# Out-projection tiles grouped 1 0 4, 3 5 8, 2 6 7, and the first up step cut at column 256

## What is computed

```python
mix = concat([gmlp_out, attn])                     # (tokens, 1024)
mix = einsum('bte,ed->btd', mix, w_out)            # out-projection
x = layer_norm(DEEPNORM_ALPHA * x + mix, ln1_g, ln1_b)
up = einsum('btd,df->btf', x, w_up)                # 1024 -> 2 * 2816
hc = conv_b + sum(conv_w[i] * hp[:, i:i + T] for i in range(3))
g, u = hc[..., :D_FF], hc[..., D_FF:]
y = einsum('btf,fd->btd', gelu(g) * u, w_down)     # followed by a second layer_norm
```

## Time and profile before

| what | value |
|---|---|
| median of 3 runs | 2336.68 us (2334.15 to 2340.17) |
| the profiled execution | 2335.85 us, its span 2334.1 us |
| TensorE matmul busy in the span | 2217.3 us (95%) |
| VectorE, ScalarE, GpSimd busy | 1657.2 (71%), 981.3 (42%), 825.8 us (35%) |
| the chain that ended last, by engine | TensorE 73%, VectorE 15%, ScalarE 4% |

### The profile page before, as it was taken

How to read it: one execution, slowest core, us unless ns; L and a number is a source line. 1 busy time by engine, 2 the same in 40 slices (tenths; PEclk the granted TensorE clock), 3 DMA queues, 4 the chain that set the end, 5 groups by cost and what they waited for, 6 DMA issues and landing times.

```text
span 2334.1 us, 35859 instructions
## 1 busy us (share of the span) xinstructions
PE 2217.3 (95%) x14276; PEld 2012.1 (86%) x14276; DVE 1657.2 (71%) x2014; ACT 981.3 (42%) x1773; POOL 825.8 (35%) x444
## 2 busy tenths in 40 slices
PE   7999899799999999999999998988999999999996
PEld 7997677799999998888798976768999999987885
DVE  1568747788878786787636697477787777767676
ACT  3226735444344334344322376454334434443342
POOL 1115234544554450220311342354455455311311
PEclk9999989899999999999999999998999999999998
DMA  5312146122222225765552213541232222365762
GB/s 154 95 34 65 55 147 185 44 84 84 83 61 85 85 67 175 252 218 194 176 135 47 58 39 106 150 153 47 80 88 60 86 85 67 107 234 189 243 214 90
DMA packets 207974, 269.50 MB, mean 115 GB/s; under 512 B 31952, under 2 KB 166584, under 8 KB 207736
## 3 DMA queue, kind: packets, MB, share of 16 engines
q1 hardware_dynamic: 207808, 267.21, 37.3%
HBM read 217.39 MB, written 46.13 MB: 113 GB/s over the span
## 4 chain that ended last, share of the span: by engine, by line
PE 73%; DVE 15%; ACT 4%; DMA 3%; issue 2%; POOL 2%; SPq 1%; ACTq 0%; DVEq 0%; POOLq 0%
PE ps L2059 35%; PE ps L1773 14%; PE ps L1738 9%; PE ps L1998 6%; DVE rl L1423 2%; DMA wrow<-in_w_down 1%; DVE bnst L1252 1%; PE ps L1798 1%; PE ps L1877 1%; PE ps L1903 1%; DVE bt L1335 1%; PE ps L1892 1%; DVE cb L1496 1%; PE ps L1856 1%; DVE rzc L1238 1%
## 5 line engine op out<-in xcount | busy, mean ns | idle before, releaser
L2059 PE MATMUL ps<-bt,bh 128*128 128x272 f32 x3520 | 591.7, 290 | 19.7 <-issue 16.0
L2059 PEld LDWEIGHTS ps<-bt,bh 128*128 128x128 f32 x3520 | 501.8, 190 | 20.8 <-issue 20.8
L938 ACT ACTIVATE bh<-wblk 128x512 fp32r<-128x512 f32 x308 | 183.6, 624 | 511.4 <-POOL wblk L745 260.8
L2059 PE MATMUL ps<-bt,bl 128*128 128x272 f32 x1760 | 366.4, 290 | 0.0
L2059 PEld LDWEIGHTS ps<-bt,bl 128*128 128x128 f32 x1760 | 277.1, 190 | 0.0
L733 POOL TENSOR_TENSOR bl<-wblk,bh 128x512 fp32r<-128x512 f32 x98 | 164.1, 1677 | 302.4 <-ACT bh L938 302.4
L1773 PE MATMUL ps<-rh,ah 128*128 128x512 f32 x792 | 247.2, 393 | 9.5 <-DVE ah L1434 5.8
L1773 PE MATMUL ps<-rl,ah 128*128 128x512 f32 x792 | 245.2, 391 | 0.0
L2059 PE MATMUL ps<-ba,bh 128*128 128x272 f32 x1408 | 235.7, 290 | 4.7 <-DVE gu L1378 2.8
L1355 DVE TENSOR_TENSOR bl<-wblk,bh 128x512 fp32r<-128x512 f32 x210 | 171.8, 850 | 85.4 <-ACT bh L938 85.4
L1423 DVE TENSOR_TENSOR rl<-wrow,rh 128x1024 fp32r<-128x1024 f32 x132 | 191.5, 1452 | 50.8 <-ACT rh L994 50.3
(11 more groups left out here) (223 smaller groups left out, 4091.8 us busy)
## 6 DMA issues: line engine op xcount, KB each, us to landing
wrow<-in_w_down SPq DMA_DIRECT2D x132, 512.0 KB, 4.6
wblk<-in_w_up SPq DMA_DIRECT2D x88, 512.0 KB, 5.2
a_scr<-hg SPq DMA_DIRECT2D x44, 552.0 KB, 3.4
araw<-a_scr SPq DMA_DIRECT2D x88, 192.0 KB, 4.3
wrow<-in_w_out SPq DMA_DIRECT2D x48, 256.0 KB, 5.4
wrow<-in_w_out SPq DMA_DIRECT2D x24, 512.0 KB, 4.6
wraw<-in_w_in SPq DMA_DIRECT2D x10, 1024.0 KB, 5.9
z_scr<-rzc SPq DMA_DIRECT2D x16, 512.0 KB, 4.7
```

Source lines behind the costliest of these rows:

```text
L938: act.activation(bh[b][:], block_of(f, b), ACT.Copy).then_inc(S["u_hi"], 1)
L2059: e = nc.tensor.matmul(out[:, n, :], lhs, rhs[:, HW_ // 2 * n:HW_ // 2 * n + HW_ // 2], start=(k == 0 and m == 0), stop=(k == HK - 1 and m ...
```

## The change

The groups become (1, 0, 4), (3, 5, 8), (2, 6, 7), so the last group holds one tile that needs a single operand and two that need four subtractions. `M_OPS` and `M_AT` follow: the first two pieces of the input are three tiles' in four pieces instead of two, tiles 2 and 3 go in one piece. In the first up step the 544 columns are cut at 256 instead of 272: columns 0 to 255 of all operands come from tiles 0, 1, 4, 5 and the samples alone. The products' first parts (12 matmuls of 256 columns) are issued ahead of what the last three tiles are needed for, their second parts (12 of 288) behind it. The second tile of the last group is turned into banks 4 and 5. ScalarE brings the first tile back ahead of the root for the third; VectorE's subtractions and low parts of the last group are put in another order; c11 goes ahead of the last three low parts; the sum for block S4 goes behind the low part of block S2 on GpSimd; `B_11` of step 1 waits for c21 instead of c22, since the banks are other ones. Each layer does all of it once.

```diff
-C3 = [(0, 1, 2), (3, 4, 8), (5, 6, 7)]
+C3 = [(1, 0, 4), (3, 5, 8), (2, 6, 7)]
...
 def up_bank(f, product):
+    if f == 0 and product in (B_S3, B_22):
+        return 6 if product == B_S3 else 2
     return 2 * ((7 * f + product) % 3)
+def z_bank(t):
+    return 4 if t == C3[2][1] else 6
...
-M_OPS = [(4, 8, 0, 3), (0, 4, 0, 3), (0, 8, 3, 4), (0, 8, 4, 5), (0, 8, 5, 8), (0, 8, 8, 9)]
+M_OPS = [(4, 8, 0, 2), (4, 8, 4, 5), (0, 4, 0, 2), (0, 4, 4, 5), (0, 8, 2, 4), (0, 8, 5, 8), (0, 8, 8, 9)]
...
+        def up_half(f, product, n):
+            bank, cut = up_bank(f, product), up_cut(f)
+            if f == 0:
+                return ps[:, bank, 512 - cut:512] if n == 0 else ps[:, bank + 1, 0:HW_ - cut]
+            return ps[:, bank + n, 0:HW_ // 2]
```

In GpSimd's queue:

```diff
-                for b in (B_S1, B_S2, B_S4):
-                    sum_up(l, 0, b)
-                for b in (B_S2, B_S1, B_22):
-                    lo_up(l, 0, b)
+                sum_up(l, 0, B_S1)
+                sum_up(l, 0, B_S2)
+                lo_up(l, 0, B_S2)
+                sum_up(l, 0, B_S4)
+                lo_up(l, 0, B_S1)
+                lo_up(l, 0, B_22)
```

In ScalarE's queue, behind the last group:

```diff
                 deviation(l, 0, t1)
                 normal(l, t1)
+                turned(l, t0)
                 deviation(l, 0, t2)
                 normal(l, t2)
-                turned(l, t0)
-                operand_hi(l, t0, 0)
                 block_hi(l, 0, B_S2)
                 turned(l, t1)
-                operand_hi(l, t1, 0)
+                operand_hi(l, t0, 0)
                 block_hi(l, 0, B_S1)
                 turned(l, t2)
+                operand_hi(l, t1, 0)
+                snap(l, 0)
+                block_hi(l, 0, B_22)
                 operand_hi(l, t2, 0)
-                for part in (1, 2):
-                    for t in C3[2]:
-                        operand_hi(l, t, part)
-                    if part == 1:
-                        snap(l, 0)
-                        block_hi(l, 0, B_22)
+                operand_hi(l, t1, 1)
+                operand_hi(l, t2, 1)
                 block_hi(l, 0, B_S3)
+                operand_hi(l, t1, 2)
+                operand_hi(l, t2, 2)
```

In VectorE's queue, behind the last group's moments:

```diff
-                    for t in C3[g]:
-                        operands(l, t)
-                for t in C3[2]:
-                    sum_third(l, t)
-                for part in (1, 2):
-                    for t in C3[2]:
-                        operand_lo(l, t, part)
+                    if g < 2:
+                        for t in C3[g]:
+                            operands(l, t)
+                turned(l, t0)
+                turned(l, t1)
+                operand_sums(l, t1, (0, 1))
+                operand_lo(l, t0, 0)
+                turned(l, t2)
+                operand_sums(l, t2, (0, 1))
+                for t in (t1, t2):
+                    operand_sums(l, t, (2,))
+                    dve.wait_ge(S["t_sum"], ts_n(l, t, 2))
+                    operand_lo(l, t, 0)
+                for t in (t1, t2):
+                    operand_sums(l, t, (3,))
+                operand_lo(l, t1, 1)
+                dve.wait_ge(S["t_sum"], ts_n(l, t2, 3))
+                joined(l, 0, "c11")
+                operand_lo(l, t2, 1)
+                for t in (t1, t2):
+                    operand_lo(l, t, 2)
```

In TensorE's queue, the first up step and the first wait of the second:

```diff
+                turn_z(l, t0)
+                times(0, B_11, b11, (0,))
+                turn_z(l, t1)
+                times(0, B_12, b21, (0,))
+                turn_z(l, t2)
+                times(0, B_S2, t2_, (0,))
+                times(0, B_11, b11, (1,))
+                times(0, B_12, b21, (1,))
+                times(0, B_S1, t1_, (0,))
+                times(0, B_S2, t2_, (1,))
+                times(0, B_S1, t1_, (1,))
+                times(0, B_S3, t3_, (0,))
+                times(0, B_S3, t3_, (1,))
+                times(0, B_22, t4_)
+                times(0, B_S4, b22, (0,))
+                times(0, B_S4, b22, (1,))
...
+                    if f == 1:
+                        pe.wait_ge(S["u_c21"], n)
```

More of the change, by code:

```diff
@@ L129, in xo_n @@
     if t in last:
-        n += 3 * part + last.index(t)
+        n += last.index(t) if part == 0 else 1 + 2 * part + last.index(t) - 1
     else:
@@ L893, in operand_hi @@
                     act.wait_ge(S["kv_out"], 32 * (l + 1))
-                elif t == HK and part == 0:
-                    act.wait_ge(S["c_done"], l * NTOK + 6)
+                elif t in (HK, HK + 1) and part == 0:
+                    act.wait_ge(S["c_done"], l * NTOK + 3 * (t - HK + 1))
                 if t < HK:
@@ L929, in block_hi @@
                     act.wait_ge(S[name], count)
-                else:
-                    act.wait_ge(S["z_tr"], (l + 1) * NTOK)
-                    for q in range(3):
-                        act.wait_ge(S[f"z_out{q}"], 16 * 3 * (l + 1))
-                    if b == B_S4:
-                        act.wait_ge(S["u_u2"], l * FT + 1)
+                elif b == B_S4:
+                    act.wait_ge(S["u_u2"], l * FT + 1)
+                else:
+                    q = b - B_S3
+                    act.wait_ge(S["z_tr"], l * NTOK + 7 + q)
+                    act.wait_ge(S[f"z_out{q}"], 16 * 3 * (l + 1))
                 act.activation(bh[b][:], block_of(f, b), ACT.Copy).then_inc(S["u_hi"], 1)
@@ L1098, in body @@
                 m_hi(l, 0)
+                m_hi(l, 1)
                 o_evac(NB - 1)
                 zu_gelu(1)
-                m_hi(l, 1)
+                m_hi(l, 2)
                 for g in range(3):
@@ L1340, in operands @@
                     operand_lo(l, t, 0)
[L1341 to L1349 removed]
+                else:
+                    operand_sums(l, t, range(4))
+                    dve.wait_ge(S["t_sum"], ts_n(l, t, 3))
                     for part in range(3):
@@ L1670, in body @@
                         conv_gate(l, f - 1)
-                    joined(l, f, "c11")
                     if f:
+                        joined(l, f, "c11")
                         conv_up(l, f - 1)
@@ L2047, in body, with times @@
                 b22 = [(bt[:, k, :], bt[:, 20 + k, :]) for k in range(HK)]
-                t1, t2, t3, t4 = ([(bt[:, 4 + 4 * i + k, :], bt[:, 24 + 4 * i + k, :]) for k in range(HK)] for i in range(4))
-                def times(f, b, right):
+                t1_, t2_, t3_, t4_ = ([(bt[:, 4 + 4 * i + k, :], bt[:, 24 + 4 * i + k, :]) for k in range(HK)] for i in range(4))
+                def times(f, b, right, halves=(0, 1)):
                     pe.wait_ge(S["u_lop" if on_pool(f, b) else "u_lov"], lo_n(l, f, b))
-                    out = up_ps(f, b)
+                    cut = up_cut(f)
                     for k in range(HK):
@@ L2057, in times @@
                         for m, (lhs, rhs) in enumerate(((lh_, rh_), (lh_, rl_), (ll_, rh_))):
-                            for n in range(2):
-                                e = nc.tensor.matmul(out[:, n, :], lhs, rhs[:, HW_ // 2 * n:HW_ // 2 * n + HW_ // 2],
+                            for n in halves:
+                                e = nc.tensor.matmul(up_half(f, b, n), lhs, rhs[:, cut:HW_] if n else rhs[:, 0:cut],
                                                      start=(k == 0 and m == 0), stop=(k == HK - 1 and m == 2))
-                    e.then_inc(S["u_p"], 1)
+                    if 1 in halves:
+                        e.then_inc(S["u_p"], 1)
                 def rows_turn(f):
```

138 lines of the change are left out of this document (70 added, 68 removed).

## The result

The changed kernel takes 2341.68 us (median; 2337.88 to 2347.6), the kernel before 2338.02 beside it (2332.01 to 2340.23): ratio 1.0021, 95% interval 1.0013 to 1.0030. By the ratio that is 4.9 us more, between 3.0 and 7.0; the medians lie 3.7 apart. The forecast was 7.4 more, with 2340 to 2347 as its own range. The profiled execution has a span of 2337.1, 3.0 over that of before. It took 2338.89 and is one of the five fastest of the twenty; the slowest, 2347.6, ran at a mean granted clock of 0.977 against its 0.982.

A forecast was written before the change was run, and what follows sets the result against it. VectorE, not TensorE, was taken to set the end of each layer's first up step. Per layer 1.3 + 2.9 - 2.3 + 0.6 = +2.5, twice 5.0, with the clock +7.4 on 2335.85: 2343.3 us, range 2332 to 2349.

The forecast's parts named there:

- Group 0: First tiles: M_OPS in four pieces starts TensorE about 1 us earlier; costed at nothing, as TensorE waits for caches.
- Step 1: End of group 1: VectorE's longer work on tile 4 moves all of group 2 by +1.3 us a layer.
- Step 2: Group 2: tile 5's wider low parts and two changed VectorE-GpSimd meetings cost +2.9 us a layer.
- two meetings named: Group 2: GpSimd rows hold VectorE's third low part and tile 8's subtractions, for 2.4 us each.
- The rival without these meetings: Group 2: GpSimd's row arrives after VectorE's third low part, so 0.0 there; total 2337.5 us; chance 0.25.
- Step 3: First up step to u2: less VectorE work but more GpSimd meetings, -2.3 us a layer.
- The five meetings: First up step to u2: VectorE waits for five GpSimd instructions, put at 5.9 us a layer together.
- faster rival: VectorE's tail to u2 loses its waits for GpSimd, -8.2 us there; total 2329.0 us; chance 0.15.
- Step 4: From u2 to TensorE's up step 1: chain to c22 keeps its length, waiting for c21 adds +0.6 us.
- The first parts of the products: First up step: they fill TensorE's idle time but are worth nothing, since the next step waits for VectorE.
- Clock: TensorE's longer wait ahead of up step 1 slows the product behind it: +2.4 us for both layers, bounds -1.6 and +3.2.
- The sum: Whole kernel: +2.5 us a layer, twice 5.0, with the clock +7.4, giving 2343.3 us.

The follow-up runs named there:

- e6: Changed kernel with tile 4's three low parts moved behind the first scaling of the second group; 2338.51 us, ratio 1.0009 to the kernel before.
- e5: Changed kernel with tile 5's third low part moved behind the moments of the last group's third tile; 2336.16 us, ratio 0.9996 to the kernel before.
- e9: Changed kernel with GpSimd's sum for block S4 put back ahead of the low part of block S2; 2336.01 us, ratio 0.9999 to the kernel before.
- e1: Changed kernel with joins u3, c22, c21 of the first up step ahead of VectorE's two low parts for the next; 2337.08 us, ratio 0.9997 to before.
- e3: Changed kernel with the first up step's products issued whole, after all three tiles are turned; 2344.89 us, ratio 1.0036 to the kernel before.
- e2: Kernel before, with joins u3, c22, c21 of the first up step ahead of VectorE's two low parts; 2332.40 us, ratio 0.9980 to the kernel before.
- e7: Changed kernel with 20 unused filler matmuls in TensorE's idle time ahead of up step 1, each layer; 2339.99 us, ratio 1.0020 to the kernel before.

## Why the prediction was right, and where not

**Group 0**, put at nothing: in layer 0 its first residual comes at 314.24 against 314.11. Right.

**Step 1**, +1.3: 1.28 (364.37 less 363.09, of which 0.13 stood already at group 0), and e6 takes 1.29 back. Right.

**Step 2**, +2.9: 2.45 (A, 41.05 less 38.60), by the two meetings named. e5 takes 1.6 to 1.7 of it back, and all of it but for the clock. Right, 0.45 too high. The rival without these meetings is out.

**Step 3**, -2.3: -2.85 (B, 33.39 less 36.24). The first turn comes 0.17 later behind the residual, as forecast, and from it u2 comes 3.0 sooner (23.13 less 26.15); the forecast's 23.9 holds that later turn, so 23.7 was its figure from the turn on. The five meetings came, at 418.98, 420.73, 428.08, 429.90 and 435.57, but they cost 4.9 together and not 5.9: the rows less 0.69, 0.69, 0.69, 1.23 and 1.23. The faster rival's mechanism exists, though not in the changed kernel, where none of the five was missed: e9 moves one line, two of them fall beside the turns, and the kernel is level with the one before. That is not the rival's 2329, whose sum takes all five as gone; no run here has that.

**Step 4**, +0.6: 12.47 us from u2 to step 1 (438.81 to 451.28) against 11.90, in layer 1 0.32 more. Right, and for its reason: c22 comes 11.08 behind u2 (449.89), 11.15 before, since the change removes nothing there. What the prediction did not ask is whether c21 has to stand there. The "chain" is partly an order in VectorE's queue; e1 shortens u2 to c21 by 6.0.

**The first parts of the products**, "so this is worth nothing", and "nothing either" if their cover is gone. This failed. They bring B_11's product early enough for ScalarE's new order; without them u2 comes 2.0 later a layer (e3). I had looked at TensorE's queue and not at ScalarE's.

**Clock**, +2.4 for both layers: mis-sized. The first product of step 1 takes 5.6 us in both, 0.96 more than in layer 0 before and 2.5 more than in layer 1; with the second product 1.2 and 2.6, in all 3.8, over the forecast's upper bound of 3.2. But in layer 1 part of it is handed back: the second c12 of the layer comes 6.4 us later than before (1629.39 against 1623.01), the last one 5.2 (2054.86 against 2049.68). In the kernel before TensorE still met VectorE on the way (0.22 us for c22 at 1664.97; its steps from step 2 to step 5 take 21.28 to 21.65 us, the changed kernel's 21.27 or 21.28). That is part of it; for the rest no run shows a cause. I had no term for it.

One more term I had not named. TensorE's wait for the third residual of group 1 is longer by step 1 (2.19 in the changed kernel against 1.01) and can halve the clock as well. TensorE's timeline of e9, where it did, and windows of e9 and of the changed kernel from about the end of that wait:

```profile
374.27 1.89 PE L2046 MATMUL ps<-rh,mrow 128*128 128x512 f32 x4 [2.20 <-DVE rzc L1272]
```

```profile
374.00:378.00 4.00, 3.73 (x9) 2.94 (x10) 1.93 (x6) 1.93 (x2) 0.69 (x1) 0.57 0.63 226
```

```profile
372.00:376.00 4.00, 3.28 (x17) 2.52 (x18) 1.85 (x6) 2.01 (x2) 0.62 (x1) 1.00 0.65 220
```

The four matmuls take 1.89 where the changed kernel's profile has 1.19, at a granted clock of 0.57 instead of 1.00, and A is 41.88 there instead of 41.05. Of the seven traces with a wait of 2.2 us in that place, six (all but the changed kernel's own) have these four matmuls at 1.86 to 2.08 us in one layer or both, 10 of 14 layers in all. In the seven with a wait of 1.0 (the kernel before, e2 and all with tile 4's low parts moved) none has. So step 1 can cost 0.8 a layer more than its 1.3, and that the profile of the changed kernel shows nothing of it is luck.

**The sum.** In layer 0 group 0, the four steps and the clock add up to 0.1 + 1.15 + 2.45 - 2.85 + 0.57 + 1.2 = 2.6, and its last c12 comes 2.6 later (901.08 against 898.46). At layer 1's it is 5.2. In the tail TensorE waited 2.07 us at 2283 in the kernel before and its clock fell; in this profile of the changed one it waited 1.60 and the clock stayed. That gives 2.1 to 2.2 back and leaves the 3.0 between the spans. The ratio's 4.9 lies near the 5.2, but with one profile of each no run shows what the other executions gained or lost. The four steps together gave 1.3 us in layer 0 and 1.15 in layer 1 where 2.5 a layer were forecast, and the clock cost 3.8 where 2.4 were: the two errors go against each other, so that the total came as near as it did is in part luck.

The Trainium skill, page "SBUF — State Buffer", section "Who interferes with whom", has a VectorE instruction with two SBUF inputs and a GpSimd instruction that reads SBUF lock each other out, for whole instructions. e9 agrees: with the two GpSimd instructions beside PSUM reads, two subtractions fall from 1.72 and 1.64 to 0.69.

## What to carry to other kernels

When one engine's instruction moves, lay its new time beside what the engine that cannot run beside it does then: a 1.3 us sum on GpSimd put among VectorE's subtractions cost 2.0 us a layer, and beside PSUM reads nothing. Before a row of waits is called a chain, ask of each instruction which data it needs; c21 stood behind two low parts that it doesn't read, and moving it paid in both kernels. Work that is not needed soon (third low parts) belongs in the waits behind the residuals, not ahead of them.

## What I had not expected

The gain of e7 is seen in both up steps, and is not in its time. Between layer 0's last c12 and layer 1's first residual of group 2 its profile takes 662.9 us where the changed kernel's takes 658.2; 0.8 of that is A. The granted clock falls in other places there. Windows of 20 us from 280 and from 320 behind the last c12, the changed kernel's first, then e7's:

```profile
1181.08:1201.08 20.00, 17.72 (x118) 17.34 (x117) 8.70 (x10) 6.51 (x10) 0.36 (x1) 1.00 0.82 190
...
1221.08:1241.08 20.00, 18.26 (x112) 18.04 (x111) 6.26 (x9) 4.81 (x8) 3.85 (x3) 0.98 0.09 31
```

```profile
1179.81:1199.81 20.00, 17.72 (x108) 17.34 (x107) 8.63 (x10) 5.04 (x8) 0.00 (x0) 0.91 0.83 195
...
1219.81:1239.81 20.00, 18.26 (x101) 18.04 (x100) 6.35 (x10) 2.36 (x4) 5.61 (x3) 0.87 0.18 57
```

Busy times are the same, but the trace has 108 and 101 matmuls instead of 118 and 112, at 0.91 and 0.87 instead of 1.00 and 0.98. e1 loses 4.0 us in the same stretch. The edits touch nothing there. Whether the clock's place follows from when the up phase ends, or is each execution's chance, no run here settles; e7's 2.6 us a layer are read only in the trace.
